# Two-block transformer on one core: TensorE reads the surplus count ahead of the last sorted expert turn

## What is computed

```python
logits = (xt @ w_router + b_router)
top_v, top_e = lax.top_k(logits, TOP_K)        # 4 of 32
gates = jax.nn.softmax(top_v, axis=-1)
...
def expert_block(args):
    xb, e = args
    return clamped_swiglu(xb @ w1[e] + b1[e]) @ w2[e] + b2[e]
...
y = jnp.zeros((T, D)).at[row_tok].add(yb * row_gate[:, None])
```

## Time and profile before

| | us |
|---|---|
| median of 3 runs | 2458.53 |
| the runs | 2449.63, 2894.22, 2458.53 |
| profiled execution, device time | 2445.24 |
| its span, first to last instruction | 2443.5 |
| PE busy | 2234.3 (91%) |
| DVE busy | 1409.2 (58%) |
| mean granted TensorE clock | 0.974 |

### The profile page before, as it was taken

How to read it: one execution, slowest core, us unless ns; L and a number is a source line. 1 busy time by engine, 2 the same in 40 slices (tenths; PEclk the granted TensorE clock), 3 DMA queues, 4 the chain that set the end, 5 groups by cost and what they waited for, 6 DMA issues and landing times.

```text
span 2443.5 us, 40909 instructions
## 1 busy us (share of the span) xinstructions
PE 2234.3 (91%) x16818; PEld 1533.7 (63%) x16818; DVE 1409.2 (58%) x2720; ACT 625.9 (26%) x778; POOL 111.3 (5%) x195
## 2 busy tenths in 40 slices
PE   6998989989988999989999998999989999987998
PEld 4887843445445454345455455777679987765987
DVE  2355455434344444564455457666697757677876
ACT  0211121222122122111112112444434423333332
POOL 0000010000000000000000000000000000000000
PEclk9999989999999999999999999999999999998999
DMA  8778889999999999999999997444355523232651
GB/s 337 307 297 342 315 307 386 403 417 400 406 398 384 413 415 419 420 416 383 382 418 419 418 417 294 164 149 153 121 197 199 185 76 115 92 120 89 224 188 68
DMA packets 111249, 711.82 MB, mean 291 GB/s; under 512 B 12480, under 2 KB 13136, under 8 KB 36128
## 3 DMA queue, kind: packets, MB, share of 16 engines
q1 hardware_dynamic: 85904, 616.93, 64.1%
q0 software_dynamic: 25168, 92.38, 10.0%
HBM read 705.06 MB, written 4.19 MB: 290 GB/s over the span
## 4 chain that ended last, share of the span: by engine, by line
PE 72%; DVE 18%; DMA 4%; ACT 3%; issue 3%; DVEq 0%; SPq 0%; ACTq 0%
PE bank L310 20%; PE bank L2241 7%; PE bank L2222 6%; PE bank L1954 5%; PE bank L1992 4%; PE bank L1969 3%; PE bank L1616 3%; PE bank L1473 2%; PE bank L2107 2%; DMA ring<-in_units_a 2%; PE bank L2326 2%; PE bank L2096 1%; PE bank L1875 1%; PE bank L2138 1%; PE bank L2308 1%
## 5 line engine op out<-in xcount | busy, mean ns | idle before, releaser
L310 PE MATMUL bank<-hid,scratch 128*32 128x512 f32 x960 | 313.5, 595 | 0.9 <-DMA hT<-in_panels_e 0.9
L310 PE MATMUL bank<-hT,scratch 128*32 128x512 f32 x928 | 307.9, 597 | 0.0
L1248 ACT CAST chi<-craw 128x1024 fp32r<-128x1024 f32 x128 | 133.3, 1044 | 504.4 <-DMA craw<-in_panels_m 218.5
L3229 DVE TENSOR_TENSOR clo<-craw,chi 128x1024 fp32r<-128x1024 f32 x128 | 156.1, 1222 | 134.3 <-ACT chi L1248 133.0
L310 PE MATMUL bank<-cst,scratch 128*32 128x512 f32 x752 | 172.3, 599 | 5.6 <-DMA yacc<-in_panels_e 5.6
L310 PE MATMUL bank<-yacc,scratch 128*32 128x512 f32 x768 | 175.8, 597 | 0.0
L310 PE MATMUL bank<-diag_gtmp,scratch 128*32 128x512 f32 x768 | 173.9, 594 | 0.0
L310 PE MATMUL bank<-rows,scratch 128*32 128x512 f32 x752 | 170.4, 595 | 0.0
L1954 PE MATMUL bank<-cT_hi,chi 128*128 128x256 f32 x384 | 114.4, 298 | 20.8 <-DVE clo L3229 8.2
L1954 PE MATMUL bank<-cT_lo,chi 128*128 128x256 f32 x384 | 111.1, 289 | 0.0
L1954 PE MATMUL bank<-cT_hi,clo 128*128 128x256 f32 x384 | 111.1, 289 | 0.0
(11 more groups left out here) (665 smaller groups left out, 5791.1 us busy)
## 6 DMA issues: line engine op xcount, KB each, us to landing
hid<-in_panels_e SPq DMA_DIRECT2D x96, 1024.0 KB, 12.0
hT<-in_panels_e SPq DMA_DIRECT2D x94, 1024.0 KB, 11.9
ring<-in_units_a SPq DMA_DIRECT2D x88, 1024.0 KB, 7.2
ring<-in_panels_m SPq DMA_DIRECT2D x64, 1024.0 KB, 5.1
yacc<-in_panels_e SPq DMA_DIRECT2D x48, 1024.0 KB, 10.7
diag_gtmp<-in_panels_e SPq DMA_DIRECT2D x48, 1024.0 KB, 10.8
rows<-in_panels_e SPq DMA_DIRECT2D x47, 1024.0 KB, 9.9
cst<-in_panels_e SPq DMA_DIRECT2D x47, 1024.0 KB, 11.3
```

What stands on the lines that cost most here:

```text
L310: m = self.pe.matmul(b[s:s + STRIP, :], lhs(k)[:, s:s + STRIP], v, start=(first and k == 0), stop=(k == KT - 1))
L1248: act.copy(chi[:, h % 2, :], context_raw(h)).then_inc(cx_hi, 1)
L3229: tt(context_lower(h), context_raw(h), chi[:, h % 2, :], ALU.subtract).then_inc(cx_lo, 1)
```

## The change

The body of the last sorted turn becomes a function, `last_turn`. PE waits for the count and loads it before that turn. Where there is a surplus, it does the last turn and then the loop of surplus turns; the counts are set back to what they were before the last turn; and where there is none (the count is under 1), it does the last turn from a second copy of its instructions. Only PE's program is changed.

```diff
-            for i in range(TURNS):
+            for i in range(TURNS - 1):
                 expert_turn(SHARES[i], turn=i, point=POINTS * i)
-            static = [x.c.n for x in fillers]
+            counted = (EG.c, EG.others, EG.panels, EA.c, EH.c, EM.c, from_experts.c)
+            before_last = [c.n for c in counted]
+
+            def last_turn():
+                expert_turn(SHARES[-1], turn=TURNS - 1, point=POINTS * (TURNS - 1))
+
             pe.wait_ge(count_ready, 1)
             more = pe.value_load(more_i[0:1, 0:1], min_val=0, max_val=MORE)
             with pe.If(more > 0):
+                last_turn()
                 with turns(pe, more, counts) as i:
                     expert_turn(SHARES[0])
                 for x in fillers:
                     x.read()
-            for x, n in zip(fillers, static):
-                x.c.n = n
+            for c, n in zip(counted, before_last):
+                c.n = n
+            with pe.If(more < 1):
+                last_turn()
+            for x in fillers:
                 x.read()
             pe.wait_ge(last_ready, 1)
```

## The result

Over 14 runs of each kernel, the changed kernel has a median of 2454.94 us and the kernel before one of 2450.77; the ratio of the two is 1.0032, with a 95% interval from 1.0018 to 1.0046. By the ratio the change makes the kernel slower by 7.8 us (4.4 to 11.3), well under the 2% at which a difference would matter; the two medians as they stand are only 4.2 us apart. One run of the kernel before, 2894.22 us, lies far above all the others and has no part in the ratio.

What follows compares the result with a forecast made beforehand. In the expert turns PE and DMA are both nearly full, so PE stalls are paid. Terms 0 + 2.7 + 1.7 - 0.4 give +4.0 us on a 2451.1 us base, so 2455 us, range 2443 to 2470.

Steps and rivals of the forecast that it cites:

- What bounds the kernel: In the expert turns PE and the DMA engines are both nearly full, so PE standing still there is paid unless swallowed.
- the old jump at 0: Between last sorted turn and combination: removing PE's jump over the surplus turns gives 0, at most 0.24 us.
- Load and wait at 0: Ahead of the last turn: the count was signalled long before, so the wait costs nothing; the 0.9 us load fits PE's lead.
- second branch at 0.2: Ahead of the last turn: the added branch, not taken, costs 0.2 us with its gap.
- The stall at 2.7 us: Start of the last turn, line 1889: PE stalls 2.7 us because the first branch jumps to instructions not at hand, taking 4.056 us.
- the rival on the slower side: Same place: the instruction fetch stands behind the panel loads, adding 8.7 us; 13.1 us in all, 2464 median; chance 0.10.
- The clock at 1.7 us: Behind the stall in the last turn: PE's clock drops to half, costing 1.7 us, bounds 0 and twice 1.7.
- Swallowed: 0.4: Last turn's 0.9 us PE wait on a `craw` load: the load may land sooner, giving back 0.4 us, at most 0.9.
- The sum: Whole change: 0 + 2.7 + 1.7 - 0.4 = +4.0 us; the forecast of 2 to 6 us slower had chance 0.62.
- The hidden stall: Start of the last turn: a branch of 0.24 us fits inside PE's 2.7 us queue lead; median 2451; chance 0.24.
- the small gain: Before the combination: the old jump is on the path after all, giving at most 0.24 us; median 2451; chance 0.04.

Runs made afterwards that it cites:

- the kernel with six jumps: Kernel before, with the old jump over the surplus-turn loop put ahead of each of the last six sorted turns, surplus turns left out; ratio 1.0117 to the kernel before.

## Why the prediction was right in its kind and wrong in its size

*What bounds the kernel, and the old jump at 0.* Right. The kernel without any branch repeats the stretch to the hundredth.

*Load and wait at 0, second branch at 0.2.* Right; the second branch took 0.083 us.

*The stall at 2.7 us.* Its place and its cause were right, its size was not: 4.5 us. The term that failed is the length of the branch, "I take the 4.056 us of the one row that shows this very jump". It was this very jump, but not in this surrounding: DMA share 0.21 there, 1.02 here. The prediction saw that the engines are full at the new place and put this into the rival on the slower side, with a price of 8.7 us taken from a load of 512 KB. The branch was longer by 2.0. That rival names the mechanism that fits the rows, with four times the price; the forecast took none of it. (Its sum, 13.1, also leaves out the -0.4. The forecast's own stall, 1402.3 less 1399.73, is 2.6 and was rounded up to 2.7.) A value between them was to be had only from a second row, and the kernel before has just the one.

*The clock at 1.7 us.* Wrong in size: 2.8. This stall was followed by 6.8 us at half clock, where the waits in the earlier trace rows were followed by 3.4 or less. The length of the stall alone doesn't set this: behind the same 5.0 us wait ahead of the combination the half level lasted some 3.4 us in the kernel before and in the one without a branch, and 6.8 in the kernels with the load alone or a short branch ahead. The price of one such stretch, 1.7 us, was read rightly, but the last sorted turn had one already (behind its 2.4 us wait), and that one stayed: in the changed kernel the clock is at half again from 1432.8 to 1436.2. In the last turn of the kernel with six jumps there was one such stretch in all, behind the 3.6 us stall and none behind the 2.4 us wait, and the turn from line 1889 to the combination took 109.5 us, nearly as before (109.3). So the clock's share in a stall of about 4 us was 0.2 us here and 2.8 there.

*Swallowed: 0.4.* Wrong, 0. The wait of 0.9 us stayed, although the load behind it did come early: the chain of the changed kernel has no DMA piece in this turn. There the chain goes from PE's piece on line 1992 (1465.75) through DVE's additions (1467.38) to PE's line 1954 (1469.57), and that way is as long. A wait can hang on two things at once; taking one away then gives nothing.

*The sum.* +4.0 was forecast; the stretch gives +7.2, the ratio of the runs +7.8 (4.4 to 11.3). The forecast lies just under the interval. The time of 2455 us is what was measured (2454.94), but this agreement is luck: it was reached from a base of 2451.1 for the kernel before (right: its median over 14 runs is 2450.77), and set beside the 2458.53 of the first three runs it is a gain, where the text forecast a loss and a loss was measured. With executions 15 to 19 us apart, three of them don't fix a base to which 4 us can be added.

*The hidden stall and the small gain.* Both fell. The 108 ns that the Trainium skill ("Advanced Engine Details and Errata", Control Flow Timing) gives for a compare-and-branch are nearest to the branches that fall through (0.076 to 0.093 us), under the near taken ones (0.21 to 0.48 us), and are some 30 times under the bare price of a far one, 3.33 us.

## What to carry to other kernels

A runtime branch costs by what has to be fetched, not by where it stands in the text: let the common case fall through, and put the rare case's instructions where only the rare case jumps. If a far jump can't be avoided, put it behind the longest queued work or under a wait that is there anyway, as the kernel before had done; and before moving a cost off a place, check on the chain of waits that the place pays for it at all. A duration read from a single row may hold only for the load of the DMA engines in that row.

## What was not expected of the hardware

- A jump forward is near or far, with a step between 128 and 256 matmuls with their weight loads: 0.2 to 0.5 us on one side, 5.9 to 6.4 on the other with DMA full, however far.
- The far jump's length goes with the DMA load when its packet of instructions is due: 3.3 to 4.1 us with a share of 0.05 to 0.3 in the branch's second microsecond, 5.0 us and more with 0.88 or more. The branch ends 1.3 to 1.5 us after the packet is in, in all 34.
- A packet of the running text that is under way holds the target's up too: 4.6 and 5.1 us at the old place.
- A far jump can stall PE twice: a second gap of 1.0 to 3.2 us, when the instructions that came with the target are used up before the next packet is in.
- The stall of PE drains the DMA engines too, as the loads are released by PE: share 0.37 some 6 us behind it.
